# Layer boundaries and the last norm tile by tile, x scaled in its transposing product, tokens of layer 2 by parity in the operands

## The reference

```python
for i in range(DEPTH):
    mod = cond @ mod_w[i] + mod_b[i]
    shift, scale, gate = jnp.split(mod[:, None, :], 3, axis=-1)
    h = rms_norm(x, norm_w[i]) * (1.0 + scale) + shift
    j = i // N_MIXERS
    if i % N_MIXERS == 0:
        y = dilated_mixer(h, a_w_in[j], slopes) @ a_w_out[j]
    else:
        y = moba_mixer(h, b_w_in[j], slopes) @ b_w_out[j]
    x = x + gate * y
return rms_norm(x, final_norm_w)
```

## Time and profile before

| | us |
|---|---|
| time, median of 3 runs | 2520.18 (2519.95 to 2521.34) |
| profiled execution, its own time | 2524.24 |
| its span | 2521.2 |
| PE busy | 2480.6 (98%) |
| PEld busy | 2118.2 (84%) |
| DVE busy | 1697.1 (67%) |
| ACT busy | 1214.1 (48%) |
| POOL busy | 43.0 (2%) |

### The profile page before, as it was taken

The page is one execution under the profiler, slowest core; times in us unless marked ns, Lnnn a source line. Parts: engine busy times, 40 slices in busy tenths (PEclk is TensorE's granted clock), DMA queues, the critical chain, the costliest instruction groups (busy, mean ns, idle before and its releaser), DMA issues.

```text
span 2521.2 us, 32917 instructions
## 1 busy us (share of the span) xinstructions
PE 2480.6 (98%) x13110; PEld 2118.2 (84%) x13110; DVE 1697.1 (67%) x2146; ACT 1214.1 (48%) x1641; POOL 43.0 (2%) x51
## 2 busy tenths in 40 slices
PE   8999999999999999999999999999999989999998
PEld 7798888888888887888888888888888878888786
DVE  5887865677777776666566766666665666666665
ACT  5557664544445445444444444444454454444543
POOL 1100000000000000000000000000000000000000
PEclk9999999999999999999999999999999999999999
DMA  6545545687767775887587677767745557767654
GB/s 219 166 143 151 150 138 188 194 269 241 248 217 247 267 251 177 261 262 240 168 255 254 194 248 237 232 206 253 247 137 184 193 172 227 225 220 223 201 193 140
DMA packets 336456, 531.92 MB, mean 211 GB/s; under 512 B 16440, under 2 KB 190848, under 8 KB 336176
## 3 DMA queue, kind: packets, MB, share of 16 engines
q1 hardware_dynamic: 335104, 526.06, 65.7%
q0 software_dynamic: 896, 3.20, 0.4%
q10 hardware_dynamic: 304, 0.57, 0.1%
HBM read 527.67 MB, written 2.10 MB: 210 GB/s over the span
## 4 chain that ended last, share of the span: by engine, by line
PE 65%; issue 29%; DVE 3%; ACT 2%; POOL 0%; DMA 0%; POOLq 0%; SPq 0%; DVEq 0%; ACTq 0%
PE proj L973 20%; PE proj L974 10%; PE proj L985 9%; PE proj L987 9%; PE proj L986 8%; PE att L1034 1%; DVE w_lo L1659 1%; PE att L1017 1%; ACT w_hi L1261 1%; PE att L1080 1%; PE att L1164 1%; PE proj L992 1%; PE proj L994 1%; PE proj L993 1%; DVE slot L1783 0%
## 5 line engine op out<-in xcount | busy, mean ns | idle before, releaser
L1659 DVE TENSOR_TENSOR w_lo<-raw,w_hi 128x1024 fp32r<-128x1024 f32 x808 | 981.5, 1218 | 611.4 <-ACT w_hi L1261 608.9
L1261 ACT ACTIVATE w_hi<-raw 128x1024 fp32r<-128x1024 f32 x808 | 848.8, 1053 | 781.6 <-PE proj L974 419.5
L973 PE MATMUL proj<-h,w_hi 128*128 128x512 f32 x2688 | 960.1, 401 | 0.0
L974 PE MATMUL proj<-h,w_lo 128*128 128x256 f32 x2688 | 752.7, 280 | 0.0
L985 PE MATMUL proj<-w_hi,h 128*128 128x512 f32 (+1 forms) x1800 | 719.6, 400 | 9.8 <-DVE w_lo L1659 4.7
L987 PE MATMUL proj<-w_hi,h 128*128 128x512 f32 (+1 forms) x1800 | 701.1, 389 | 0.0
L986 PE MATMUL proj<-w_lo,h 128*128 128x512 f32 (+1 forms) x1800 | 699.6, 389 | 0.0
L973 PEld LDWEIGHTS proj<-h,w_hi 128*128 128x128 f32 x2688 | 505.1, 188 | 120.2 <-issue 0.5
L974 PEld LDWEIGHTS proj<-h,w_lo 128*128 128x128 f32 x2688 | 507.4, 189 | 1.3 <-issue 0.7
L985 PEld LDWEIGHTS proj<-w_hi,h 128*128 128x128 f32 x1800 | 339.6, 189 | 79.1 <-issue 8.3
L987 PEld LDWEIGHTS proj<-w_hi,h 128*128 128x128 f32 x1800 | 338.9, 188 | 71.9
(11 more groups left out here) (232 smaller groups left out, 1463.1 us busy)
## 6 DMA issues: line engine op xcount, KB each, us to landing
raw<-in_a_w_in SPq DMA_DIRECT2D x320, 512.0 KB, 4.6
raw<-in_mod_w SPq DMA_DIRECT2D x192, 512.0 KB, 4.2
raw<-in_w_in_odd SPq DMA_DIRECT2D x128, 512.0 KB, 4.5
raw<-in_b_w_in SPq DMA_DIRECT2D x128, 512.0 KB, 4.1
raw<-in_w_in_even SPq DMA_DIRECT2D x96, 512.0 KB, 3.7
raw<-in_w_out_even SPq DMA_DIRECT2D x32, 512.0 KB, 3.7
raw<-in_w_out_odd SPq DMA_DIRECT2D x32, 512.0 KB, 5.2
raw<-in_a_w_out SPq DMA_DIRECT2D x32, 512.0 KB, 3.9
```

Of the source, the lines that this page charges most:

```text
L973: pe.matmul(both, hi[:, kk, ws], x.rearrange("p two n -> p (two n)"), start=u.first and kk == 0, stop=False)
L974: done = pe.matmul(both[:, 0:SEQ], lo[:, kk, ws], x[:, 0, :], start=False, stop=u.last and kk == WIDE_K - 1)
L1261: act.activation(m.w_hi[u.n % SPLIT_N][:, 0:size], m.raw[i][:, 0:size], ACT.Copy).then_inc(s.hi_ready, 1)
L1659: dve.tensor_tensor(m.w_lo[ring][:, 0:size], m.raw[i][:, 0:size], m.w_hi[ring][:, 0:size].bitcast(F32), ALU.subtract).then_inc(s.lo_dve, 1)
```

## The change

**Start.** The first two k-tiles of x and the first unit's weights by k-tile come in transfers of their own, with the other two k-tiles of x behind them; the first unit's split is in two items, `split` and `split_rest`. `rows2` moves from slot 1 to slot 4.

**Boundaries of layers 2 and 3.** `resid` at the end of a layer becomes `tail`, one item for each tile. `tile_sum` sums one tile's squares, POOL raises that one column, and `diag` multiplies the identity by the norms of that tile: a matrix with the norms on its diagonal. `turn` (two k-tiles of one tile of x) and `hin` use that matrix as the moving operand of a plain product, which scales and transposes at once; `xn` and the scaled copy in `mixed` are gone. The first two units of these layers are run as four `part` items, six products for one tile each: unit 0 tile 0, unit 1 tile 0, unit 0 tile 1, unit 1 tile 1. ACT and DVE make the halves of each pair and tile in `turn` and `low`. The splits of the later units move from e + 0.5 to e + 0.9, behind all of these.

**Last norm.** `final` is one item for each tile, behind that tile's own sum.

**Parity in layer 2.** `h` stays in the order of the tokens. The values of the second and third group and the gate `z` (12 chunks of form "token") are `by_parity`: their stationary operand is every second column of `h`. The scores take every second column of the queries as stationary operand, and of the keys of groups two and three as moving operand. The keys and values of the first group stay in the tokens' order, and its mask is rewritten to match.

```diff
+    heads = []
     for p in range(PAIRS):
         m = len(h["last"])
         free = h["last"][m - H_RING] + 1 if m >= H_RING else 0
         slot = boundary + 0.1 + 0.2 * p if p < HEAD_PAIRS else first + p - HEAD_PAIRS
...
-        it = plan.at(slot, "hin", layer=layer, pair=p, n=m, banks=(m % 4,), h_free=free)
-        if p == 0 and layer != 1:
-            it.fine = max(layer, 1)
-            it.banks = (m % 4, (m + 2) % 4)
-            plan.units[first].fine = it.fine
-        if layer >= 2:
-            plan.at(boundary if p < HEAD_PAIRS else boundary + 0.2 if p == HEAD_PAIRS else slot - 1, "xn", item=it)
+        if layer >= 2 and p < HEAD_PAIRS:
+            heads.append((plan.units[first + p], m, free))
+            plan.units[first + p].head = True
+        else:
+            it = plan.at(slot, "hin", layer=layer, pair=p, n=m, banks=(m % 4,), h_free=free)
+            if p == 0 and layer == 0:
+                it.fine = 1
+                it.banks = (m % 4, (m + 2) % 4)
+                plan.units[first].fine = 1
...
+    if heads:
+        head_units(plan, layer, boundary, heads)
...
+def head_units(plan, layer, e, heads):
...
+    turns = {}
+    for tile in range(TILES):
+        for p, (unit, m, free) in enumerate(heads):
+            turns[p, tile] = Item(layer=layer, tile=tile, pair=p, unit=unit, n=m, h_free=free, banks=(2 * p + tile,),
+                                  ready=2 * tile + p + 1)
+    plan.at(e + 0.15, "turn", item=turns[0, 0])
+    plan.at(e + 0.25, "low", item=turns[0, 0])
+    plan.at(e + 0.30, "turn", item=turns[1, 0])
+    plan.at(e + 0.40, "low", item=turns[1, 0])
+    plan.at(e + 0.45, "part", item=turns[0, 0])
+    for p in range(HEAD_PAIRS):
+        plan.at(e + 0.50 + 0.1 * p, "turn", item=turns[p, 1])
+        plan.at(e + 0.55 + 0.1 * p, "low", item=turns[p, 1])
+    plan.at(e + 0.70, "part", item=turns[1, 0])
+    plan.at(e + 0.75, "part", item=turns[0, 1])
+    plan.at(e + 0.80, "part", item=turns[1, 1])
...
-                c = plan.chunk(2, 4, w, k * D + g * CHUNK, "token", "slot", **place)
+                c = plan.chunk(2, 4, w, k * D + g * CHUNK, "token", "slot", by_parity=k > 2, **place)
...
-        zs.append(plan.chunk(2, 4, w, 9 * D + g * CHUNK, "token", "slot", slot=11, func=ACT.Silu, col=g * CHUNK,
+        zs.append(plan.chunk(2, 4, w, 9 * D + g * CHUNK, "token", "slot", slot=11, func=ACT.Silu, col=g * CHUNK, by_parity=True,
...
-            plan.at(c.last if c.tail else c.last + 1, "resid", chunk=c, layer=c.layer, n=c.col // CHUNK)
+            if c.tail:
+                plan.at(c.last, "tail", chunk=c, layer=c.layer, n=c.col // CHUNK, tile=0)
+                plan.at(c.last + 0.1, "tail", chunk=c, layer=c.layer, n=c.col // CHUNK, tile=1)
...
-        plan.at(e + 2 if l < 2 else e, "sum", layer=l)
...
-    plan.at(1, "rows2", banks=(3,))
+            continue
+        for tile in range(TILES):
+            it = plan.at(e + (0.05, 0.2)[tile], "tile_sum", layer=l, tile=tile, n=TILES * (l - 2) + tile + 1)
+            if l < LAYERS:
+                plan.at(e + (0.08, 0.35)[tile], "diag", item=it)
+            else:
+                plan.at(e + (0.3, 0.5)[tile], "final", item=it)
+    plan.at(4, "rows2", banks=(3,))
...
-            slot += 0.5
+            slot += 0.9
         plan.at(slot, "split", unit=u)
+        if u.n == 0:
+            plan.at(slot + 0.15, "split_rest", unit=u)
...
+def tensor_part(pe, w, m, s, plan, it):
...
+    w.wait_ge(s.lo_dve, u.n + 1)
+    if it.ready < 2 * HEAD_PAIRS:
+        w.wait_ge(s.head_low, (2 * HEAD_PAIRS - 1) * (it.layer - 2) + it.ready)
+    else:
+        w.wait_ge(s.h_done, it.n + 1)
...
+    x_hi, x_lo = (m.rows_of(h, it.tile) for h in m.halves(it.n % H_RING))
+    ring = u.n % SPLIT_N
+    o = m.proj[c.n % 2][:, it.tile * CHUNK:(it.tile + 1) * CHUNK]
+    for kk in range(UNIT_K):
+        w_hi, w_lo = (a[ring][:, columns(kk)] for a in (m.w_hi, m.w_lo))
+        pe.matmul(o, x_hi[:, kk], w_hi, start=u.first and kk == 0, stop=False)
+        pe.matmul(o, x_hi[:, kk], w_lo, start=False, stop=False)
+        done = pe.matmul(o, x_lo[:, kk], w_hi, start=False, stop=False)
+    if it.tile == TILES - 1:
+        done.then_inc(s.unit_done, 1)
+
...
     c = u.chunk
+    if u.head:
+        return
...
+                t_hi, t_lo = (m.rows_of(h, tile)[:, kk] for h in (x_hi, x_lo))
+                if c.by_parity:
+                    t_hi, t_lo = (m.parity(h[:, kk, :], tile) for h in (x_hi, x_lo))
+                pe.matmul(o, t_hi, hi[:, kk, :], start=start, stop=False)
+                pe.matmul(o, t_hi, lo[:, kk, :], start=False, stop=False)
+                done = pe.matmul(o, t_lo, hi[:, kk, :], start=False, stop=stop)
...
+        q = m.feature(plan.slot_of[it.layer, it.group, "q", g])[:, h, :]
+        k = m.feature(plan.slot_of[it.layer, it.group, "k", g])[:, h, :]
+        q = m.parity(q, it.tile) if it.layer == 2 else q[:, own]
+        k = m.parity(k, it.tile) if g else k[:, cols]
...
-                    done = pe.transpose(m.bank(it.banks[j if it.fine else 0], at, at + P), src[:, tile, k * P:(k + 1) * P], m.ident)
+                    turned = m.bank(it.banks[j if it.fine else 0], at, at + P)
+                    x = m.x_res[:, tile, k * P:(k + 1) * P]
+                    if it.layer < 2:
+                        done = pe.transpose(turned, x, m.ident)
+                    else:
+                        done = pe.matmul(turned, x, m.rstd_diag[:, tile, :], start=True, stop=True)
...
+        elif kind == "turn":
+            w.wait_ge(s.tile_diag, TILES * (it.layer - 2) + it.tile + 1)
+            for j in range(UNIT_K):
+                k = it.pair * UNIT_K + j
+                done = pe.matmul(m.bank(it.banks[0], j * P, (j + 1) * P), m.x_res[:, it.tile, k * P:(k + 1) * P],
+                                 m.rstd_diag[:, it.tile, :], start=True, stop=True)
+            if it.ready < 2 * HEAD_PAIRS:
+                done.then_inc(s.turn_mm, 1)
+            else:
+                done.then_inc(s.h_mm, HEAD_PAIRS)
...
+                w.wait_ge(s.raw_first, 16)
+                act.activation(m.w_hi[0][:, columns(0)], m.raw[0][:, columns(0)], ACT.Copy).then_inc(s.hi_first, 1)
+                continue
             w.wait_ge(s.raw_landed[i], 16 * use)
...
             ring = u.n % SPLIT_N
+            if u.n == 0:
+                w.wait_ge(s.hi_first, 1)
+                dve.tensor_tensor(m.w_lo[0][:, columns(0)], m.raw[0][:, columns(0)], m.w_hi[0][:, columns(0)].bitcast(F32),
...
+            dve.tensor_reduce(m.row_rstd[:, 0, it.tile:it.tile + 1], m.square_sums[:, it.tile, :], AXIS_X,
+                              ALU.add).then_inc(s.tile_sum, 1)
+        elif kind == "diag":
+            w.wait_ge(s.tile_rstd, it.n)
+            dve.tensor_scalar(m.rstd_diag[:, it.tile, :], m.ident, m.rstd(it.tile), None, ALU.mult).then_inc(s.tile_diag, 1)
...
+        elif kind == "low":
+            hi, lo = (m.rows_of(h, it.tile) for h in m.halves(it.n % H_RING))
+            w.wait_ge(s.turned, it.dve_n)
+            if it.ready < 2 * HEAD_PAIRS:
+                w.wait_ge(s.head_hi, (2 * HEAD_PAIRS - 1) * (it.layer - 2) + it.ready)
+            else:
+                w.wait_ge(s.h_hi, it.n + 1)
+            done = dve.tensor_tensor(lo, m.rows_of(m.val(it), it.tile), hi.bitcast(F32), ALU.subtract)
+            if it.ready < 2 * HEAD_PAIRS:
+                done.then_inc(s.head_low, 1)
+            else:
+                done.then_inc(s.h_done, HEAD_PAIRS)
...
-    sp.dma_start(m.x_res[:, :, columns(0)], x[:, :, columns(0)]).then_inc(s.x_landed[0], 16)
+    near, far = slice(0, UNIT_K * P), slice(UNIT_K * P, CHUNK)
+    sp.dma_start(m.x_res[:, :, near], x[:, :, near]).then_inc(s.x_first, 16)
...
+        if j == 0:
+            c = u.chunk
+            for k in range(UNIT_K):
+                src = c.w[k * P:(k + 1) * P, c.col0:c.col0 + c.width]
+                landed = s.raw_landed[0] if k == UNIT_K - 1 else s.raw_first
+                sp.dma_start(m.raw[0][:, columns(k)], src).then_inc(landed, 16)
+            sp.dma_start(m.x_res[:, :, far], x[:, :, far]).then_inc(s.x_landed[0], 16)
+            continue
```

269 lines of the change are left out of this document (149 added, 120 removed).

## The result

The changed kernel took **2527.11 us** (median of 9 runs, 2526.24 to 2528.02) where the kernel before took 2520.18 (9 runs beside it, 2518.46 to 2521.53): 1.0027 times as long, 95% interval 1.0019 to 1.0035. It is slower by 6.9 us, where 2518.0 was forecast with a range up to 2522.0. The profiled execution took 2526.67 at a span of 2524.9.

What follows compares the result with a forecast made beforehand. Matrix products cover 98% of the span, so only TensorE's stalls, half clock and the two ends could save; DVE and ACT bound the heads. 1.7 + 0.4 - 0.7 + 0.84 = 2.2 us off 2520.18 gave 2518.0, range 2514.8 to 2522.0.

Steps and rivals of the forecast that it cites:

- I take 0 and keep the rival below: Layer 2: step-two stationary operands in 1152 products and 96 score loads cost 0, judged by the recurrence's moving operand.
- strided weight loads: Rival, chance 0.08: step-two loads take twice as long, 96 score loads cost 10.4 us, 1152 others stay hidden: 2528.4.
- Four transposes took 0.60 and eight plain products 1.05, 0.11 for each of the four more: Layers 2 and 3: the price of scaling x in a plain product instead of scaled copy and transpose; costed at nothing.
- the chain of 3.78: Heads of layers 2 and 3: pairs follow 3.78 us apart, bound by DVE and ACT, TensorE waiting.
- The start: First product near 8.5, sixth unit's wait ending at 30.5; 2.5 us gained, 0.8 if the clock falls, 1.7 taken.
- The boundary of layer 2: Head of layer 2: first product 2.9 us sooner, mostly melting into a wait before the third unit; 0.4 us gain taken.
- the fourth ends at 956.0: Head of layer 2: the fourth half-pair ends at 956.0, so DVE starts the next splits at 956.5, not 957.08.
- the 0.85 of the kept clock: Head of layer 2: gain of 0.85 us at full clock; the rival of a clock kept everywhere (2515.3) had chance 0.13.
- The boundary of layer 3: Head of layer 3: first product near 2022.3, half clock likelier, +0.7 us at full clock; a loss of 0.7 taken.
- 0 to 1.6 lost: Head of layer 3 at half clock: pair 2 starts on DVE at 2030.6 to 2032.2, against 2030.58 before.
- The end: Last norm by tile: the output transfers leave 0.84 us sooner, which nothing behind can take back.
- I take the differences as equal in both: Base: profiled execution some 4 us slower than the runs, taken alike for both kernels, so 2.2 came off the median 2520.18.

Runs made afterwards that it cites:

- experiment 1: The kernel before, unchanged, run and traced once more: 2520.41 us, ratio 1.0001; its trace has a span of 2518.7.
- experiment 2: The changed kernel with the 12 chunks of layer 2 reading contiguous columns of h, scores still at step two: 2519.88 us, ratio 0.9999.
- experiment 5: The kernel before with all step-two operands, but third group's values read at step four and the gate at step eight: 2533.86 us (one run).
- experiment 12: The change with contiguous chunk operands, turns of tile 1 and pair 2 earlier, later splits of units 6 to 8 and later low halves: 2516.12 us, ratio 0.9983.
- experiment 4: The kernel before with only the start edits and the last norm by tile: 2518.54 us, ratio 0.9993.
- experiment 9: The kernel before with start edits, last norm by tile, and splits of units 6, 7 and 8 half a slot later: 2516.65 us, ratio 0.9986.
- experiment 8: The kernel before with the start edits alone: 2519.91 us, ratio 0.9999.
- experiment 7: The change with contiguous chunk operands and the turns of tile 1 ahead of the first six products: 2522.80 us, ratio 1.0009.
- experiment 11: The change with contiguous chunk operands, tile 1's turns ahead of the first six products, pair 2's ahead of the last twelve: 2518.01 us, ratio 0.9992.
- experiment 6: The kernel before with start edits, last norm by tile, and x scaled in its transposing product, both tiles together: 2519.07 us, ratio 0.9995.
- experiment 10: The kernel before with start edits, last norm by tile, later splits of units 6 to 8, and halves one slot later from pair 2: 2511.42 us, ratio 0.9965.
- experiment 3: The kernel before with all step-two operands of layer 2, chunks and scores, and nothing else of the change: 2527.30 us, ratio 1.0028.

## Why the prediction was wrong

Trace of the change against that of experiment 1, in us, + for slower. The columns are what the prediction took for the part and the shift of TensorE's work over it:

| part | predicted | measured |
|---|---|---|
| start | -1.7 | -2.8, of it about 1.7 kept clock |
| head of layer 2 | -0.4 | +0.2 |
| 12 chunks by parity | 0 | +7.4 |
| wide sections | 0 | -0.9 |
| head of layer 3 | +0.7 | +2.4 |
| end | -0.84 | -0.4 |

The measured parts sum to 5.9 of the 6.2 us between the spans.

**Edits costed at nothing: the step that failed.** The step is "I take 0 and keep the rival below", for the stationary operand of 1152 products at step two. It measured 7.4 us, 6.6 ns a product: the whole loss against the kernel before, and most of the 9.1 us by which the forecast missed. Without it the change takes 2519.88 (experiment 2). The 0 stood on the moving operand of the recurrence, which is another operand, and the prediction itself said that no row shows the one in question. The rival "strided weight loads" then had the right cause and the wrong place. It held that a load of 0.11 hides under a product of 0.227 until it takes 2.1 times as long, and so priced the 96 score loads at 10.4 us and the 1152 others at nothing. It is the reverse. The products of 512 columns, whose loads lie beside them, come 6.6 ns later each, and the score products cost some 0.9 in all. That a longer load hides is nearly right (experiment 5: 0.117 more of load at step four, 1.7 ns more between products), but not wholly, and a few per cent on each of 1152 products is all that the loss needs. Why they come is not shown. The forecast gave this rival 0.08, for a price that no row bounded; with that price open, the slower end belonged in the range.

**The scaling product.** "Four transposes took 0.60 and eight plain products 1.05, 0.11 for each of the four more" compared records, not products: the eight records were four products. The right price is 0.42 a pair. Behind the chain of 3.78 it stayed unseen in the change, so this slip did not move the forecast; it shows once the chain is shortened (experiment 12).

**The start.** First product 8.28 (8.5 predicted), no wait at the third unit, one of 2.34 at the sixth (about 2): right. Other traces with the new start have the first product anywhere from 7.45 to 9.06, and those of experiments 4 and 9 do wait at the third unit, for 1.4 and 1.6. The weights landed at 25.9, not 27.4, so that unit came at 29.19 instead of 30.5. The gain was 0.4 by medians (experiment 8) where 1.7 was taken, but the interval there includes 1.7. What did fail is the way there: it took the old clock loss of the earlier trace rows as given and kept the new one for even odds, while both starts sometimes keep the clock and sometimes lose it.

**The boundary of layer 2.** First product 2.6 us sooner against the tail (2.9 predicted), 1.7 of waiting before the third unit (about 3 predicted), pairs 3.78 apart as said. But "the fourth ends at 956.0" was 1.1 too early. Measured from tile 0's addition, DVE began the splits 11.35 us later where the step gives 10.35, because it waited 0.57 for tile 1's turns behind the first six products, and its rounds were longer (tile 1's diagonal stands in one). So the 0.85 of the kept clock, which it did keep, became nothing: +0.2. Experiment 1 had the clock at 0.50 for 6.8 us at this head (950.9 to 957.7), and its pair 2 was no later.

**The boundary of layer 3.** First product 2.2 sooner (2.0 predicted; 2.0 against the trace that it read), half clock as taken, from 2025.0 to 2028.4. The loss is 2.4, not 0.7. Against the trace that the prediction read it is 1.5, inside its "0 to 1.6 lost", since the old head took 33.0 there and 32.1 in experiment 1. But that range counted products ahead of pair 2 only. The same half clock stretches the six products ahead of tile 1's turns, and DVE waits 2.17 there. The Trainium skill (TensorE: Matmul & The Clock Gate, Part 4) would have plain products count as work where transposes do not. Here the turns are plain, and the clock stayed full in layer 2 and fell to 0.50 in layer 3, so they don't secure it.

**The end.** 0.88 sooner to the last issue (0.84 predicted). "Which nothing behind it can take back" is not borne out: from that issue to the end of the span it is 6.4 us in the change and in experiments 2, 7, 11 and 12, which have the boundaries by tile, and 5.9 in the kernel before and in all the others, whichever end they have. So half a microsecond of the 0.88 is lost again in the last transfers; why is not known.

**The base.** "I take the differences as equal in both" put the trace's 2524.24 beside the median and found 4 us of slowness. The second trace, at 2520.83, shows that most of these lay in a few places, and terms rest on two of them, the start and the head of layer 3.

**What stays open.** Two wide sections of layer 2 take 101.04 us in experiment 1 and 100.41 in the change. In experiment 1 the first of them runs between these two products (the change is shown above, 1412.44 to 1512.85):

```profile
1412.09 0.47 PE L973 MATMUL proj<-h,w_hi 128*128 128x512 f32 x1
...
1513.14 0.40 PE L985 MATMUL proj<-w_hi,h 128*128 128x512 f32 x1
```

All traces split the same way: 101.04 in the kernel before and experiments 1, 4, 6, 8, 9 and 10, which write the tokens reordered, 100.4 in the change and experiments 2, 3, 5, 7, 11 and 12, which leave them in order and read the scores at step two. So that part of the change also wins back 0.6 in each of the two and loses 0.4 in an earlier section, 0.9 in all. Which of its edits does so, and why, wasn't found. That earlier section also differs by 1.07 between two executions of the kernel before.
